# Six weight loads of the second feed forward queued ahead of the last four chunks of the cross attention

## What is computed

```python
for l in range(DEPTH):
    h = layer_norm(ALPHA * h + 0.5 * swiglu(h, ffn1...), ...)
    z = h @ w_in[l]            # short conv, recurrence (hgrn2), pooling on parts of z
    mix = concatenate([y_conv, y_rec, y_pool]) @ w_out[l]
    h = layer_norm(ALPHA * h + mix, ...)
    h = layer_norm(ALPHA * h + cross_attn(h, mem, ca_q, ca_k, ca_v, ca_o), ...)
    h = layer_norm(ALPHA * h + 0.5 * swiglu(h, ffn2...), ...)   # d_ff = 2816
```

## Time and profile before

| | us |
|---|---|
| median of 3 runs | 3273.83 |
| lowest, highest | 3273.67, 3275.25 |
| profiled execution, its own time | 3278.56 |
| its span in the profile | 3276.7 |
| TensorE busy in it | 3069.0 |

### The profile page before, as it was taken

The page is one execution under the profiler, slowest core; times in us unless marked ns, Lnnn a source line. Parts: engine busy times, 40 slices in busy tenths (PEclk is TensorE's granted clock), DMA queues, the critical chain, the costliest instruction groups (busy, mean ns, idle before and its releaser), DMA issues.

```text
span 3276.7 us, 39679 instructions
## 1 busy us (share of the span) xinstructions
PE 3069.0 (94%) x13191; PEld 2182.0 (67%) x13201; DVE 2132.5 (65%) x4320; ACT 953.8 (29%) x2506; POOL 1222.6 (37%) x1136
## 2 busy tenths in 40 slices
PE   9999999999999999999999999978999999987777
PEld 7688888887887888887886845533435855542224
DVE  7877787765555456874555696567565587577544
ACT  2320011221001002221002464334446464443333
POOL 1003545343444442453430144433443044444432
PEclk9999999999999999999999999999999999999999
DMA  9787988787998996788996899999999899999998
GB/s 361 257 282 279 375 345 312 280 339 302 353 351 339 360 348 234 259 331 306 365 354 239 322 421 420 420 420 392 407 421 419 308 420 420 420 421 422 422 422 351
DMA packets 252469, 1164.47 MB, mean 355 GB/s; under 512 B 27304, under 2 KB 34952, under 8 KB 186400
## 3 DMA queue, kind: packets, MB, share of 16 engines
q0 software_dynamic: 153792, 828.44, 62.9%
q1 hardware_dynamic: 98480, 334.10, 28.2%
q10 hardware_dynamic: 48, 0.05, 0.0%
HBM read 1161.39 MB, written 1.10 MB: 355 GB/s over the span
## 4 chain that ended last, share of the span: by engine, by line
PE 68%; DMA 17%; DVE 6%; ACT 5%; issue 2%; POOL 0%; SPq 0%; ACTq 0%; DVEq 0%; POOLq 0%
PE ps_b L1534 18%; PE ps_a L1471 14%; DMA ring<-in_peer_uv,idx 12%; PE ps_a L1542 9%; PE ps_b L787 7%; PE ps_a L774 4%; ACT arena L1770 3%; DMA arena<-in_peer_uv,idx 2%; DMA wring<-in_second_w 2%; PE ps_b L1299 2%; DVE ring L2966 2%; DMA ring<-in_ffn 1%; PE ps_b L1292 1%; PE ps_b L1237 1%; ACT L1770 1%
## 5 line engine op out<-in xcount | busy, mean ns | idle before, releaser
L1471 PE MATMUL ps_a<-ring,arena 128*128 128x512 f32 x1728 | 819.9, 609 | 129.4 <-ACT arena L1770 128.8
L749 POOL DMA_INDIRECT ring<-in_peer_uv,idx x448 | 493.3, 1101 | 886.6 <-PE ps_a L1471 628.0
L2966 DVE SCALAR_TENSOR_TENSOR ring<-ring,h_tm 128x1024 f32<-128x1024 f32 x448 | 547.0, 1224 | 379.4 <-DMA ring<-in_peer_uv,idx 378.6
L712 POOL DMA_INDIRECT ring<-in_peer_uv,idx_now x512 | 580.3, 1133 | 415.0 <-DVE arena L2784 165.6
L1471 PEld LDWEIGHTS ps_a<-ring,arena 128*128 128x128 f32 x1728 | 308.4, 191 | 560.7 <-ACT arena L1770 289.0
L1534 PE MATMUL ps_b<-x_t,ring 128*128 128x256 f32 x2816 | 623.4, 380 | 3.4 <-DMA ring<-in_ffn 2.4
L1534 PEld LDWEIGHTS ps_b<-x_t,ring 128*128 128x128 f32 x2816 | 532.6, 190 | 83.0 <-DMA ring<-in_ffn 4.3
L1770 ACT ACTIVATE arena<-ps_b 128x256 f32<-128x256 f32 (+3 forms) x218 | 99.4, 458 | 1206.2 <-PE ps_b L1534 830.6
L1542 PE MATMUL ps_a<-arena,ring 128*128 128x256 f32 x1408 | 318.7, 379 | 0.0
L2784 DVE SCALAR_TENSOR_TENSOR arena<-ring,h_tm 128x1024 f32<-128x1024 f32 x256 | 298.7, 1219 | 14.1 <-DMA ring<-in_peer_uv,idx_now 11.8
L1542 PEld LDWEIGHTS ps_a<-arena,ring 128*128 128x128 f32 x1408 | 267.2, 190 | 39.6 <-issue 3.5
(11 more groups left out here) (462 smaller groups left out, 3359.7 us busy)
## 6 DMA issues: line engine op xcount, KB each, us to landing
ring<-in_ffn SPq DMA_DIRECT2D x264, 512.0 KB, 7.4
wring<-in_second_w SPq DMA_DIRECT2D x166, 512.0 KB, 5.0
wring<-in_mix_w SPq DMA_DIRECT2D x120, 512.0 KB, 6.6
ring<-in_ada_rows POOLq DMA_DIRECT2D x44, 512.0 KB, 6.2
ring<-in_second_w SPq DMA_DIRECT2D x12, 1024.0 KB, 10.3
ring<-in_peer_uv,idx_now POOLq DMA_INDIRECT x512, 8.3
ring<-in_peer_uv,idx POOLq DMA_INDIRECT x448, 14.7
arena<-in_second_w SPq DMA_DIRECT2D x13, 512.0 KB, 11.8
```

The source lines that it names most:

```text
L712: G.indirect_dma_start(rows[:, s, :], None, table, bass.IndirectOffsetOnAxis(ap=idx_now[:, half, s:s + 1], axis=0)).then_inc(rows_in[s], p ...
L749: G.indirect_dma_start(pairs[slot].rearrange("p c d -> p (c d)"), None, a["peer_uv"], bass.IndirectOffsetOnAxis(ap=idx[:, b, s:s + 1], axi ...
L1471: ins = mm(ps_a[:, b * D + j * 512:b * D + (j + 1) * 512], diags[:, at % DIAGS, :], pairs[at % PAIRS][:, 1, j * 512:(j + 1) * 512], start= ...
L2966: V.scalar_tensor_tensor(row, row, 1.0, h_tm[:, n // SLOTS, :], ALU.mult, ALU.mult, accum_out=dots[:, n % SLOTS:n % SLOTS + 1]).then_inc(d ...
```

## The change

On SP the six loads of the second feed forward's tiles 0 and 1 are issued before the last four chunks of `mix_w`, in both layers. The rows of the modulation stay behind both.

```diff
                 for w in range(2):
-                    if w:
-                        chunk_loads(a["mix_w"], mix_at + (MIX_CHUNKS - WR), WR)
                     for ft in range(2):
                         for part in range(3):
                             ff_loads(l * (2 * FT) + (w * FT + ft), ft, part)
                     if w == 0:
                         mod_row_loads(row_at)
                     else:
+                        chunk_loads(a["mix_w"], mix_at + (MIX_CHUNKS - WR), WR)
                         mod_row_loads(row_at + 1)
                         mod_row_loads(row_at + 2)
```

## The result

The changed kernel takes 3259.14 us (median of 5 runs, 3255.24 to 3260.23), the one before 3275.25 beside it (3273.67 to 3275.8). The ratio is 0.995, 95% interval 0.994 to 0.9961, so 13 to 20 us faster. A second comparison gave 3261.55 for 3274.64, ratio 0.9959 (0.9946 to 0.9973), 13.1 us. The prediction said 13.6.

A forecast was written before the change was run, and what follows sets the result against it. TensorE, busy 94% of the span, was taken to bound the kernel, so gains must be gaps in its work. Removing wait and slow clock (14.6) less the stall (1.0) gave 13.6 off 3273.83: 3260.2 us, range 3257 to 3268.

The forecast's parts named there:

- The wait and the clock: From the output projection's last product to the mean's end: 10.72 and 11.33 us fall to 3.73, gaining 14.6.
- The undisturbed norm: The norm behind the feed forward, same instructions without a DMA wait: 3.73 us from last product to mean's end.
- The stall at chunk 56: In the output projection, chunk 56 lands late behind the six loads: 0 to 2.9 us, taken as 0.5 a layer.
- the prediction's bounds at half the bandwidth: Chunk 56 lands at 720.1 to 722.6 if SP's queue gets half beside the gather; it is needed at 722.0.
- the lower end: Of the 0 to 2.9 us stall at chunk 56, the forecast took 0.5 a layer, 1.0 in all.
- the 43.8% of the long stretch: SP queue's share against the gather from 722.4 to 729; by it chunk 56 lands at 722.4 to 724.9.
- The gather's rows: VectorE's 16 weighted sums end near 726, not 717.6, covered unless they end after some 732; cost nothing.
- The feed forward's waits: Early waits for feed forward weights, 2.4 us in all on TensorE, left unchanged with 2.4 less to 2.4 more.
- The sum: Whole kernel: 14.6 - 1.0 = 13.6 us off the median 3273.83 gives 3260.2.
- Slower: Rival: the six loads starve the output projection at a share below 32%; at 24.5%, 3293 us; chance 0.07.
- The wait under another name: Rival: the row chunk or residual still holds up the norm; gain 0 to 5, 3269 to 3274 us; chance 0.08.

The follow-up runs named there:

- the spare products: The kernel before, with 11 spare products between the output projection and the norm: 3268.96 us for 3274.31, ratio 0.9984.
- the two with the row first: The kernel before, with the first modulation row's chunks queued ahead of the six loads; two runs: 3259.84 us for 3274.31, and 3260.54 for 3274.64.
- two spare loads: The changed kernel with two more unused 512 KB loads behind the six in each layer: 3278.04 us in one execution, with before at 3273.25.

## Why the prediction was right

- *The wait and the clock, 6.99 + 7.60 = 14.6.* Measured in the stretches 6.84 + 7.61 in the first profile, with 3.73 from the last product to the mean's end in both layers. The undisturbed norm of the same kernel was the right measure. The split was seen by itself with the spare products (1.9 and 2.5 for the clock, the rest the wait).
- *The stall at chunk 56, 0.5 a layer, 1.0 in all.* The profiles with the change in place show a projection longer than 27.79 by 0.14, 0.41 and 0.81 in layer 0 (three profiles) and by 0.00, 0.01 and 0.06 in layer 1 (three). So 0.1 to 0.9 in all. Chunk 56 landed 13.8 us behind the projection's begin; the prediction's bounds at half the bandwidth were 12.0 to 14.5, and it's needed at 13.9. The chunk lands just as it's needed, here 0.1 us before, and 0.5 after in the second profile of the same kernel. That the stall isn't 3 us hangs on this, which the prediction could bound but not see: the choice near the lower end was right in part by luck. Its reason was half right too: the 43.8% of the long stretch was no share that the queue gets while it moves, it held the late start of loads beside the gather (the 0.01 MB of 724.5 to 725.5). While both queues move, SP's share in the changed kernel was 49.7 to 52% in every stretch of 4 us from 704 to 720, an even split. The Trainium skill (DMA: Bandwidth & Descriptors, "Queues, rings and completion order") says that the engines go round their queues packet by packet; the trace agrees, with 224 packets of each queue in 712 to 716:

```profile
q0 software_dynamic: 224, 0.83, 51.7%
q1 hardware_dynamic: 224, 0.82, 51.0%
```

- *The gather's rows, costed at nothing.* Right: the sums were to end near 726 on a projection from 708.08, 17.9 behind its begin, and ended 20.9 behind it, 3 later than forecast. The gather's queue has moved 3.76 MB from 700 to 720 and 0.94 more by 724, so the eight rows' 4.19 MB are through near 722, and the last sum starts at 724.17. Some 2 of the 3 us thus lie between a row's last bytes and its landing (an estimate from these numbers), which the forecast's sum didn't hold. VectorE's wait for the last pair, 4.6 us, covered it.
- *The feed forward's waits, left as they are.* 2.4 us on TensorE became 1.1 in the first profile, but 2.9 in the second one of the same kernel, and 1.2 and 2.0 in the two with the row first. So no gain can be told from them, and none was forecast.

```profile
L1533 PE MATMUL ps_b<-x_t,ring 128*128 128x256 f32 x2816 | 623.4, 380 | 2.0 <-DMA ring<-in_ffn 1.1
```

- *The sum, 13.6 off the median, 3260.2.* The measured medians are 3259.14 and 3261.55, 16.1 and 13.1 under the one before beside them. The profiled execution fell by 3278.56 - 3255.24 = 23.3, which is more than the change: its stretches explain 14.45. Of the rest 3.49 is there before anything moves, at the begin of layer 0's projection (708.08 and 704.59). The two executions also differ in the clock elsewhere: the mean granted clock of the span is 0.993 before and 0.997 after, but 0.994 in the second profile of the changed kernel, which took 3263.43 with the same stretches but for 0.7 us.
- *The rivals.* Slower was priced at a share below 32%. The share wasn't that low, but the mechanism is real: 1.05 MB more in front of chunk 56 takes all of the gain, and the same six loads issued 15 us later, between output chunks 57 and 58, take it and 7 us more. The wait under another name (rows late, residual late) didn't come.

## What to carry to other kernels

When a wait ends with a DMA, compare the time from its issue to its landing with that of a load of the same size elsewhere. If it's much longer, look at what was issued to the same queue just before, and when that was needed. There are two ways to move such loads away, ahead of a tight stretch or behind it, and both gave the same here. In front of a load with little slack, add up the bytes and divide them by the share of the bandwidth that the queue gets: here 1.05 MB made the difference between 14 us won and nothing. Add to an idle time of TensorE what the clock takes from the products behind it, by a row of the same products at full clock; here that was 1.9 and 2.5 us on top of 5.

## What had not been expected

- Beside the full gather a load on SP's queue had its first bytes some 3 us after its issue (3.6 for the chunk issued at 711.9 in the run with the six loads two chunks later), against some 0.9 on quiet engines. While the queue has older loads to move this is hidden, and the share is even. With the six loads issued 7.5 us into the projection it isn't, and the wait was 3 us longer than the bytes divided by an even share say.
- The slow clock costs 1.9 to 2.5 us behind a gap of 5 us, two fifths to a half of the gap again, and 1.7 and 2.9 in the middle of the projection with two spare loads. It was left out of two expectations, and each came out too short by it.
